# The order of residual, routing and bias products ahead of the expert loop of a hybrid decoder step

## The chip, the cores and the metric

The kernel runs on one core of one Trainium2 chip. The metric is device time in microseconds of one execution. TensorE (PE) multiplies matrices, VectorE (DVE) and ScalarE (ACT) work elementwise, GpSimd (POOL) does small odd jobs, SyncE (SP) issues the transfers. They run beside each other and meet at semaphores.

## The reference

One decoder layer for 256 prompt tokens and 32 new tokens (8 sequences of 4): norm, one projection, dilated attention beside a state-space mixer, output projection, residual, then a mixture of experts, residual, and a last norm. All in float32, D = 1024, 32 experts, 4 for each token. The part that matters here:

```python
logits = h @ w_router + b_router
top_v, top_i = lax.top_k(logits, 4);  gates = softmax(top_v)
# for each expert e and the tokens that chose it:
a = xb @ w1[e] + b1[e]                       # 1024 -> 2048
x_glu = minimum(a[:, :1024], 7);  x_lin = clip(a[:, 1024:], -7, 7)
mid = x_glu * sigmoid(1.702 * x_glu) * (x_lin + 1)
y  = mid @ w2[e] + b2[e]                     # 1024 -> 1024
out[token] += gate * y;   x = x + out;   y = rmsnorm(x) * norm_final_g
```

## The kernel before

Tokens lie in three tiles: 128 and 128 of the prompt, 32 samples (`TILES`). After the mixers comes the routing stage, then a loop over 32 experts. Each expert's weights are 12 pieces of 1 MB. There are 20 buffers for pieces (`NSLOT`); SP fills all of them with the pieces of the first experts before or during routing, and then refills a buffer each time the last block of its expert has used it (`refill`, L462 to L469). An expert works on its tokens in blocks of 32 (`CAP`), one pass of `pe_pass` each, 51 passes here. A pass gathers its tokens with a product against a selection matrix (L1572), multiplies by the first weights (`first_product`, L1592), by the second (`second_product`, L1600), and adds the block's rows to the output, which stays in PSUM banks 0 to 4 for the whole loop (`sum_back`, L1560 and L1562).

Experts are taken in an order by load: the two first are always experts 0 and 1, so that their weights can be fetched before routing is known; the others follow by their counts. Names, counts and running block numbers (`names_o`, `cnt`, `blk_n`) are read into registers by every engine that runs the loop.

The routing stage is one instruction stream for each engine, in the order of the code, with waits on semaphores. On PE: the transposes of the normed rows (L1486 to L1492), the logits (L1507), their stacking (L1512), the positions of the tokens within their expert (L1525), the counts as a row (L1528) and as a column (L1531), the gates transposed (L1535), the second bias times the gates (L1543, three groups by tile: `second_bias(0)`, `(2)`, `(1)`, with a wait between the last two), and the broadcast of names and counts to all partitions (L1548). Between them stand the products that put the residual rows x into the output banks with an identity matrix: `residual(q)` for quarter q of the columns (L1498, 512 wide, 128 rows), and four small ones for the samples (L1518, 256 wide, 32 rows). The bias products add to what the residual products wrote.

On DVE: the top-4 (L1065 to L1077, mask there at its end), the softmax (L1080 to L1083), the gates by expert (L1090), the positions by expert (L1101, L1103), the ranks and names (L1105 to L1111), the evictions of the broadcast (L1116 to L1123), and twice three copies that repeat the sample column of a table in all four quadrants of partitions (`in_all_quadrants`, L1094, for `gate` and `posm`). Then its loop begins: registers are read, and L1143 makes the first selection matrix.

Of the kernel before, what the change touches and what calls it, by code (L numbers as in the profile page):

```python
# [34 lines left out]
NS = NB * NSEQ  # L35
# [6 lines left out]
NEXP, TOPK, DFF = 32, 4, 1024  # L42
CAP = 32
NQ = D // (P // CAP)
# [76 lines left out]
def decoder_step(nc, I, O):  # L121

    with ExitStack() as ctx:
# [29 lines left out]
        ident = con[:, C_ID:C_ID + P]  # L153
# [5 lines left out]
        x = sb("x", [P, 3, D])  # L159
# [27 lines left out]
        posm = moe_buf(NEXP * 3).rearrange("p (e t) -> p e t", e=NEXP)  # L187
        gate = moe_buf(NEXP * 3).rearrange("p (e t) -> p e t", e=NEXP)
# [61 lines left out]
        ones = sb("ones", [P, P])  # L250
# [8 lines left out]
        rt_s = routing[:, 0:576].rearrange("p (t k e) -> p t k e", t=3, k=6)  # L259
# [7 lines left out]
        put = oh[0:NEXP, 0, :, :]  # L267
# [3 lines left out]
        ps = ctx.enter_context(nc.psum_tensor("ps", [P, 8, 512], F32))  # L271
# [10 lines left out]
        S = {n: sem("s_" + n) for n in names}  # L282
# [490 lines left out]
        def _(dve):  # L773
            chain = [0]

            def link(ins):

                chain[0] += 1
                ins.then_inc(S["chain_v"], 1)
                dve.wait_ge(S["chain_v"], chain[0])  # L780
# [11 lines left out]
            for t, (_, n) in enumerate(TILES):  # L792
                ins = ts(xn[0:n, t, :], x[0:n, t, :], st[0:n, 6 + t:7 + t], None, ALU.mult)
# [38 lines left out]
            q = lambda n: prm[:, n, :]  # L832
# [24 lines left out]
            for g in range(2):  # L857
# [3 lines left out]
                ins = tt(dst(1), s4(0)[rows], s4(1)[rows], ALU.add)  # L861
# [105 lines left out]
            for hh in range(H):  # L967
# [17 lines left out]
                if hh == 0:  # L985
                    sample_maxima(0)
                    dve.wait_ge(S["ysps"], 1)
                    for blk in range(4):
                        ins = stt(yS[:, blk, SEQ:], qkvu[:, 12 + blk, SEQ:], dsk[:, blk:blk + 1], ps[:, 2, NS * blk:NS * blk + NS], ALU.mult, ALU.add)
# [32 lines left out]
            for t, (_, n) in enumerate(TILES):  # L1022
                ins = ts(st[0:n, 36 + 2 * t:38 + 2 * t], ps[0:n, 5, 2 * t:2 * t + 2], 1.0 / 512, EPS, ALU.mult, ALU.add)
# [3 lines left out]
            for k, t in enumerate(SERVED):  # L1027
                n = TILES[t][1]
                dve.wait_ge(S["wo_ps"], k + 1)
                if t == 2:  # L1030
                    for a in range(2):
                        for c in range(2):
                            q = 64 * a + 32 * c
                            xv = x[0:n, t, 512 * c:512 * c + 512]
                            ins = stt(xv, ps[q:q + n, 4, :], st[0:n, 42 + 2 * t + a:43 + 2 * t + a], xv, ALU.mult, ALU.add)
# [17 lines left out]
                ins = dve.reciprocal(st[:, 54 + t:55 + t], st[:, 51 + t:52 + t])  # L1053
# [9 lines left out]
            lg, masks, es = rt_s[:, :, 0, :], rt_s[:, :, 1, :], rt_s[:, :, 2, :]  # L1063
            for t, (_, n) in enumerate(TILES):
                ins = stt(lg[0:n, t, :], ps[0:n, 6, 32 * t:32 * t + 32], st[0:n, 54 + t:55 + t], bro[0:n, :], ALU.mult, ALU.add)  # L1065
            link(ins)
            for t, (_, n) in enumerate(TILES):
                ins = dve.max(top[0:n, t, 0:8], lg[0:n, t, :])
            link(ins)
            for t, (_, n) in enumerate(TILES):  # L1070
                ins = dve.max_index(tidx[0:n, t, :], top[0:n, t, 0:8], lg[0:n, t, :])
# [14 lines left out]
            def by_expert(table, u, n):  # L1086
                return table[0:n, :, u].rearrange("p e t -> p t e")

            for u, n in ((slice(0, 2), P), (slice(2, 3), NS)):
                ins = dve.tensor_copy(by_expert(gate, u, n), es[0:n, u, :])  # L1090

            def in_all_quadrants(table):
                for q in range(1, 4):
                    ins = dve.tensor_copy(table[32 * q:32 * q + 32, :, 2], table[0:NS, :, 2])  # L1094
                return ins

            link(ins)
            in_all_quadrants(gate)

            dve.wait_ge(S["posps"], 1)  # L1100
            link(stt(rt_s[:, :, 3, :], ps[:, 7, 0:96].rearrange("p (t e) -> p t e", t=3), 1.0, masks, ALU.add, ALU.mult))  # L1101
# [8 lines left out]
            ts(put[:, 2, :], put[:, 1, :], name_col, None, ALU.mult)  # L1110
            ts(put[:, 3, :], put[:, 1, :], ps[0:NEXP, 7, 128:129], None, ALU.mult).then_inc(S["gates"], 1)  # L1111

            link(in_all_quadrants(posm))

            dve.wait_ge(S["gT_ps"], 2)
            dve.tensor_copy(names_o[:, :], ps[:, 7, 192:224])  # L1116
            ts(cnt[:, :], ps[:, 7, 224:256], 1.0, None, ALU.max).then_inc(S["cntr"], 1)
# [3 lines left out]
            link(ts(nblk[:, 0, :], nblk[:, 0, :], -ROUND, None, ALU.add))  # L1121
            link(dve.tensor_tensor_scan(nblk[:, 1, :], ones[:, 0:NEXP], nblk[:, 0, :], 0.0, ALU.mult, ALU.add))
            ts(blk_n[:, :], nblk[:, 1, :], -1.0, None, ALU.add).then_inc(S["blks"], 1)  # L1123

            def gating(n):

# [53 lines left out]
        def _(pe):  # L1180
            mm, tp = pe.matmul, pe.transpose
# [16 lines left out]
            for a, src in enumerate((par[0:NI, 0:P], par[0:NI, P:2 * P], st_out[0:NI, 0, :], st_out[0:NI, 1, :])):  # L1198
                ins = tp(ps[:, 0, NI * a:NI * a + NI], src, ident[0:NI, 0:NI])
# [3 lines left out]
            for r in range(2):  # L1203
                for b in range(4):
                    tp(ps[:, 2 + r, P * b:P * b + P], cnat[:, r, b, :], ident)
                ins = tp(ps[:, 1, P * r:P * r + P], h0row[:, r, :], ident)
# [21 lines left out]
            for r in range(2):  # L1228
                for b in range(4):
                    ins = tp(ps[:, r, P * b:P * b + P], xb[:, r, P * b:P * b + P], ident)  # L1230
# [163 lines left out]
            for i in range(NI):  # L1394
                blk, q = i // 4, 32 * (i % 4)
                for r in range(2):
                    ins = mm(ps[q:q + 32, 2, NS * blk:NS * blk + NS], cT[:, r, P * blk + q:P * blk + q + 32], hs[:, r, i, :],
                             start=(r == 0), stop=(r == 1), skip_group_check=True)
# [24 lines left out]
            for r in range(2):  # L1423
                tp(ps[0:NI, 1, P * r:P * r + P], hf[:, r, :], ident)
                ins = tp(ps[:, 1, SEQ + P * r:SEQ + P * r + P], sf[:, r, :], ident)
# [11 lines left out]
            for half in range(2):  # L1437
                for hp in range(4):
                    own = ident.rearrange("p (b r) -> p b r", b=4)[:, :, 8 * hp:8 * hp + 8]
                    at = P * half + 32 * hp  # L1440
                    ins = mm(ps[:, 0, at:at + 32], o_s[half][:, P * hp:P * hp + P], own, start=True, stop=True)
# [49 lines left out]
            for j in range(J):  # L1491
                ins = tp(ps[:, 4 + j // 4, P * (j % 4):P * (j % 4) + P], h[:, 1, j::J], ident)  # L1492
                if j % 4 == 3:
                    ins.then_inc(S["hT_ps"], 1)

            def residual(q):

                mm(ps[:, q, :].rearrange("p (t n) -> p t n", t=2), ident, x[:, 0:2, NQ * q:NQ * q + NQ], start=True, stop=True, skip_group_check=True)  # L1498

            pe.wait_ge(S["xT_a"], 4 + 4)  # L1500
            residual(0)
            pe.wait_ge(S["xT_a"], 4 + 5)
            pe.wait_ge(S["xT_d"], 4 + 1)
            for k in range(2):
# [1 line left out]
                    j = 4 * k + q  # L1506
                    ins = mm(ps[32 * q:32 * q + 32, 5, 0:NTOK], wr[:, j, :], accT[:, j, :], start=(k == 0), stop=(k == 1), skip_group_check=True)  # L1507
            ins.then_inc(S["lgT"], 1)
            residual(1)
            pe.wait_ge(S["lgs"], 1)  # L1510
            for t, (t0, n) in enumerate(TILES):
                ins = mm(ps[0:n, 6, 32 * t:32 * t + 32], lgT[:, t0:t0 + n], stack, start=True, stop=True)  # L1512
            ins.then_inc(S["lg"], 1)

            residual(2)
            residual(3)
            for q in range(4):
                mm(ps[32 * q:32 * q + 32, 4, 0:NQ], ident[0:NS, 0:NS], x[0:NS, 2, NQ * q:NQ * q + NQ], start=True, stop=True, skip_group_check=True)  # L1518

            pe.wait_ge(S["mask"], 1)  # L1520
            for t, (t0, n) in enumerate(TILES):
# [3 lines left out]
                    mm(ps[0:n, 7, 32 * t:32 * t + 32], w, rt_s[0:m, u, 1, :], start=(u == 0), stop=(u == t))  # L1525
            for u in range(3):
                m = TILES[u][1]
                ins = mm(ps[0:NEXP, 7, 96:128], ones[0:m, 0:NEXP], rt_s[0:m, u, 1, :], start=(u == 0), stop=(u == 2))  # L1528
            for u in range(3):
                m = TILES[u][1]  # L1530
                ins = mm(ps[0:NEXP, 7, 128:129], rt_s[0:m, u, 1, :], ones[0:m, 0:1], start=(u == 0), stop=(u == 2))  # L1531
            ins.then_inc(S["posps"], 1)
            pe.wait_ge(S["gates"], 1)
            for t, (t0, n) in enumerate(TILES):
                ins = mm(ps[NEXP * t:NEXP * t + NEXP, 6, 0:n], rt_s[0:n, t, 2, :], ident[0:n, 0:n], start=True, stop=True)  # L1535
            ins.then_inc(S["gT_ps"], 1)
            pe.wait_ge(S["gT"], 1)
            pe.wait_ge(S["b2"], 16 * 7)
            def second_bias(t):
                e0, n = NEXP * t, TILES[t][1]  # L1540
                for q in range(4):
                    out = ps[:, q, NQ * t:NQ * t + NQ] if t < 2 else ps[32 * q:32 * q + 32, 4, 0:NQ]
                    ins = mm(out, gT[e0:e0 + NEXP, 0:n], b2_rows[e0:e0 + NEXP, NQ * q:NQ * q + NQ], start=False, stop=True, skip_group_check=True)  # L1543
                ins.then_inc(S["comb"], 1)

            second_bias(0)
            pe.wait_ge(S["gates"], 2)
            mm(ps[:, 7, 192:256], ones[0:NEXP, :], put[:, 2:4, :], start=True, stop=True).then_inc(S["gT_ps"], 1)  # L1548
            second_bias(2)
            pe.wait_ge(S["comb"], 2)  # L1550
            second_bias(1)
            pe.wait_ge(S["cntr"], 1)

            def quarter(q):
# [121 lines left out]
```

## Time and profile before

| | us |
|---|---|
| median of 3 executions | 1273.71 (1271.83 to 1274.16) |
| profiled execution | 1274.16 |
| its span | 1272.4 |
| PE busy | 1103.0 (87%) |
| DVE busy | 428.0 (34%) |
| ACT busy | 212.4 (17%) |
| transfers, mean over the span | 350 GB/s, 442.46 MB read |
| mean granted clock of PE | 0.948 of full speed |

The page gives the busy time of each engine and a strip of 40 equal slices. The chain of waits runs back from the last instruction: PE 52%, transfers 18%, SP's queue 11%, DVE 10%. A timeline row has the start in us from the span's start, the length in us, the engine, the line of the code, the operation with out<-in by the program's names, rows*columns of the weights, the shape, and the number of instructions; a float32 product is two instructions, a transpose one. In brackets stands the idle time before it and what ended it. A windows row has the stretch, its length, the busy time of PE, of its weight loads (PEld), DVE, ACT and POOL with their number of instructions, the granted clock of PE (1.00 is 2.4 GHz), the busy share of the transfer engines, and GB/s. A row of the chain has start, length, engine, output and line. `ps` is PSUM, `x` the residual rows, `uni`, `low`, `ring`, `accT`, `tmp` and `kv_rows` are on-chip memory that is used in turn for several tables and for weights.

### The profile page before, as it was taken

How to read it: one execution, taken by the hardware profiler on the slowest of the kernel's cores; microseconds unless marked ns; L12 is line 12 of the kernel's file. 1: busy time of each engine (PE TensorE's matmuls, PEld its weight loads, DVE VectorE, ACT ScalarE, POOL GpSimd, SP SyncE). 2: the span in 40 equal slices, each digit the busy share in tenths (PEclk: the TensorE clock that was granted, in tenths of full speed). 3: DMA queues.
4: the chain of work that ended last, by engine and by line, in shares of the span. 5: the costliest groups of instructions: out<-in, count | busy, mean ns of one | idle time of the engine just before them, and what ended most of it. 6: DMA issues, size and time to landing. Idle time of an engine off the chain costs nothing.

```text
span 1272.4 us, 30002 instructions
## 1 busy us (share of the span) xinstructions
PE 1103.0 (87%) x10851; PEld 501.5 (39%) x10852; DVE 428.0 (34%) x1361; ACT 212.4 (17%) x377; POOL 80.5 (6%) x189
## 2 busy tenths in 40 slices
PE   5999788999988799989898877699899968998985
PEld 4765444453433244433343332243344412443332
DVE  4999853642222222222222211122222211222121
ACT  3102433230111111111111100011111110111112
POOL 2268400000000000000000000000000000000000
PEclk9999998989998899999999988899899998999897
DMA  8424692970799999999999999999999999999995
GB/s 245 159 83 146 190 332 93 391 303 18 303 419 420 420 415 374 419 421 382 419 421 420 420 420 420 420 369 419 421 419 384 420 419 420 385 419 420 420 420 221
DMA packets 81108, 446.25 MB, mean 351 GB/s; under 512 B 16768, under 2 KB 18112, under 8 KB 32256
## 3 DMA queue, kind: packets, MB, share of 16 engines
q1 hardware_dynamic: 81024, 445.00, 86.9%
q8 instruction: 68, 1.11, 0.4%
q14 instruction: 16, 0.13, 0.0%
HBM read 442.46 MB, written 2.51 MB: 350 GB/s over the span
## 4 chain that ended last, share of the span: by engine, by line
PE 52%; DMA 18%; SPq 11%; DVE 10%; issue 4%; ACT 1%; POOL 0%; DVEq 0%; ACTq 0%
PE ps L1592 20%; DMA ring<-in_w_moe_dram 11%; SPq L469 10%; PE ps L1600 10%; DMA low<-in_w_moe_dram 5%; PE ps L1572 4%; PE ps L1562 3%; PE ps L1585 3%; DMA w_glu<-in_w_moe_dram 2%; PE ps L1462 2%; PE ps L1580 1%; PE ps L1560 1%; PE ps L1617 1%; PE ps L1622 1%; DVE ring L892 1%
## 5 line engine op out<-in xcount | busy, mean ns | idle before, releaser
L1592 PE MATMUL ps<-ring,uni 128*32 128x512 f32 x2032 | 252.9, 636 | 76.0 <-issue 51.6
L1592 PEld LDWEIGHTS ps<-ring,uni 128*32 128x32 f32 x2032 | 63.9, 114 | 254.8 <-issue 205.2
L1128 DVE TENSOR_SCALAR uni<-ps 128x256 f32<-128x256 f32 x51 | 21.7, 425 | 336.6 <-PE ps L1592 336.6
L1600 PE MATMUL ps<-ring,uni 128*32 128x256 f32 x1792 | 105.8, 381 | 7.9 <-DMA ring<-in_w_moe_dram 7.9
L753 ACT ACTIVATE uni<-uni 128x256 f32<-128x256 f32 x51 | 21.2, 416 | 436.3 <-DVE uni L1128 436.3
L1150 DVE COPY uni<-ps 128x256 f32<-128x256 f32 x51 | 21.7, 425 | 214.4 <-PE ps L1580 214.4
L1572 PE MATMUL ps<-uni 128*32 128x256 f32 x1248 | 82.7, 401 | 0.0
L753 ACT ACT_TABLE_LOAD x51 | 65.4, 1283 | 89.3 <-issue 89.3
L1600 PEld LDWEIGHTS ps<-ring,uni 128*32 128x32 f32 x1792 | 54.6, 110 | 48.5 <-DMA ring<-in_w_moe_dram 11.7
L1221 PE MATMUL ps<-accT,ring 128*128 128x288 f32 x256 | 66.0, 413 | 0.0
L1562 PE MATMUL ps<-uni 32*128 32x256 f32 x832 | 62.9, 418 | 0.0
L1562 PEld LDWEIGHTS ps<-uni 32*128 32x128 f32 x832 | 39.5, 194 | 48.4 <-issue 46.8
L1585 PE MATMUL ps<-uni 32*32 32x512 f32 x416 | 55.1, 600 | 0.0
L1221 PEld LDWEIGHTS ps<-accT,ring 128*128 128x128 f32 x256 | 48.1, 192 | 15.6 <-issue 3.3
L1572 PEld LDWEIGHTS ps<-uni 128*32 128x32 f32 x1248 | 36.5, 113 | 38.7 <-issue 22.2
L1143 DVE TENSOR_TENSOR uni<-low,uni 128x96 f32 x51 | 13.2, 259 | 112.7 <-issue 103.0
L755 ACT ACTIVATE uni<-ps 128x384 f32<-128x384 f32 x51 | 25.0, 491 | 149.5 <-PE ps L1622 149.5
L757 ACT ACTIVATE uni<-ps 128x256 f32<-128x256 f32 x51 | 19.6, 385 | 176.1 <-PE ps L1600 176.1
L1137 DVE COPY uni<-ps 128x256 f32<-128x256 f32 x51 | 21.7, 425 | 69.9 <-PE ps L1617 69.9
L1155 DVE TENSOR_TENSOR uni<-uni 128x64 f32<-128x64 f32 x204 | 44.5, 218 | 1.4
L1592 PE MATMUL ps<-tmp,uni 128*32 128x512 f32 x320 | 41.8, 641 | 1.4 <-DMA tmp<-in_w_moe_dram 1.4
L1156 DVE TENSOR_TENSOR uni<-uni 32x32 f32<-32x32 f32 x204 | 37.0, 182 | 2.1
(378 smaller groups left out, 1287.2 us busy)
## 6 DMA issues: line engine op xcount, KB each, us to landing
ring<-in_w_moe_dram SPq DMA_DIRECT2D x232, 1024.0 KB, 24.5
tmp<-in_w_moe_dram SPq DMA_DIRECT2D x38, 1024.0 KB, 26.0
kv_rows<-in_w_moe_dram SPq DMA_DIRECT2D x19, 1024.0 KB, 23.4
w_glu<-in_w_moe_dram SPq DMA_DIRECT2D x19, 1024.0 KB, 26.7
mixer<-in_w_moe_dram SPq DMA_DIRECT2D x19, 1024.0 KB, 25.1
uni<-in_w_moe_dram SPq DMA_DIRECT2D x19, 1024.0 KB, 26.2
accT<-in_w_moe_dram SPq DMA_DIRECT2D x19, 1024.0 KB, 26.5
low<-in_w_moe_dram SPq DMA_DIRECT2D x19, 1024.0 KB, 26.9
```

The source lines that it names most:

```text
L469: sp.dma_start(slot(turn, k), piece(following[later - 1], k2)).then_inc(landed(turn, k), 16)
L753: A(sig, glu_b, ACT.Sigmoid, scale=ALPHA).then_inc(S["sgm"], 1)
L755: A(selT, ps[:, 5, 0:3 * P], ACT.Copy).then_inc(S["selT"], 1)
L1155: tt(selg[:, 0:2, q, :], sel[:, 0:2, :], gb[:, 0:2, :], ALU.mult)
L1156: ins = tt(selg[rows, 2, q, :], sel[rows, 2, :], gb[rows, 2, :], ALU.mult)
L1221: ins = mm(ps[:, 4 + n % 2, 0:NTOK], w_in[:, c // 4, j, P * (c % 4):P * (c % 4) + P], accT[:, j, :], start=(j == 0), stop=(j == J - 1))
L1462: ins = mm(ps[:, 4 * t + 2 * a + c, :], src[:, kb, t0:t0 + P], w_out[:, 4 * a + kb, 512 * c:512 * c + 512], start=(kb == 0), stop=(kb == 3))
L1562: ins = mm(ps[:, q, NQ * t:NQ * t + NQ], selT[quarter(q), P * t:P * t + P], y[quarter(q), :], start=False, stop=True, skip_group_check=True)
L1572: ins = mm(ps[quarter(q), 6, 0:NQ], sel[:, t, :], h[:, t, NQ * q:NQ * q + NQ], start=(t == 0), stop=(t == 2), skip_group_check=True)
L1585: mm(hidden(q), pick[quarter(q), :], b1_rows[quarter(q), :].rearrange("p (g n) -> p g n", g=2), start=True, stop=False, skip_group_check=True)
L1592: ins = mm(hidden(q), xe[:, k % 2, quarter(k // 2)], slot(turn, k)[:, :, NQ * q:NQ * q + NQ], start=False, stop=(k == 7), skip_group_check ...
L1600: ins = mm(ps[quarter(q), 7, 0:NQ], mt[:, m, quarter(k - 8)], slot(turn, k)[:, m, NQ * q:NQ * q + NQ], start=(k == 8 and m == 0), stop=(k ...
```

## The change

On PE, `residual(q)` takes the sample product of its quarter with it (four small products, one behind each wide one, where they stood together). Residual 0 and 1 go behind the stacked logits (ahead of the mask), residual 2 and 3 behind the counts (ahead of the transposed gates). The broadcast of names and counts goes ahead of all bias products, and the three bias groups follow each other. The wait of residual 0 on ACT's copies goes. The row of counts is made for 128 partitions where it was made for 32. On DVE the six copies of `in_all_quadrants` go from two places to one behind `blk_n`, and DVE waits for the last of them before its loop.

```diff
             for u, n in ((slice(0, 2), P), (slice(2, 3), NS)):
-                ins = dve.tensor_copy(by_expert(gate, u, n), es[0:n, u, :])
-            def in_all_quadrants(table):
-                for q in range(1, 4):
-                    ins = dve.tensor_copy(table[32 * q:32 * q + 32, :, 2], table[0:NS, :, 2])
-                return ins
-            link(ins)
-            in_all_quadrants(gate)
+                dve.tensor_copy(by_expert(gate, u, n), es[0:n, u, :])
...
-            link(in_all_quadrants(posm))
...
             ts(blk_n[:, :], nblk[:, 1, :], -1.0, None, ALU.add).then_inc(S["blks"], 1)
+            for table in (gate, posm):
+                for q in range(1, 4):
+                    ins = dve.tensor_copy(table[32 * q:32 * q + 32, :, 2], table[0:NS, :, 2])
+            link(ins)
...
-            pe.wait_ge(S["xT_a"], 4 + 4)
-            residual(0)
...
-            residual(1)
...
-            residual(2)
-            residual(3)
-            for q in range(4):
+            def residual(q):
+                mm(ps[:, q, :].rearrange("p (t n) -> p t n", t=2), ident, x[:, 0:2, NQ * q:NQ * q + NQ], start=True, stop=True, skip_group_check=True)
                 mm(ps[32 * q:32 * q + 32, 4, 0:NQ], ident[0:NS, 0:NS], x[0:NS, 2, NQ * q:NQ * q + NQ], start=True, stop=True, skip_group_check=True)
+            residual(0)
+            residual(1)
...
-                ins = mm(ps[0:NEXP, 7, 96:128], ones[0:m, 0:NEXP], rt_s[0:m, u, 1, :], start=(u == 0), stop=(u == 2))
+                ins = mm(ps[:, 7, 96:128], ones[0:m, :], rt_s[0:m, u, 1, :], start=(u == 0), stop=(u == 2))
...
             ins.then_inc(S["posps"], 1)
+            residual(2)
+            residual(3)
             pe.wait_ge(S["gates"], 1)
...
+            pe.wait_ge(S["gates"], 2)
+            mm(ps[:, 7, 192:256], ones[0:NEXP, :], put[:, 2:4, :], start=True, stop=True).then_inc(S["gT_ps"], 1)
...
-            second_bias(0)
-            pe.wait_ge(S["gates"], 2)
-            mm(ps[:, 7, 192:256], ones[0:NEXP, :], put[:, 2:4, :], start=True, stop=True).then_inc(S["gT_ps"], 1)
-            second_bias(2)
-            pe.wait_ge(S["comb"], 2)
-            second_bias(1)
+            for t in (0, 2, 1):
                 e0, n = NEXP * t, TILES[t][1]
+                if t == 1:
+                    pe.wait_ge(S["comb"], 2)
```

PE before, from the residual product ahead of the logits to the first product for the positions (`x` is the residual, `accT` the transposed rows, `low` and `uni` hold constants and logits):

```order
L1498 MATMUL ps<-x,low 128x512
L1507 MATMUL ps<-accT,low 32x288 x8
L1498 MATMUL ps<-x,low 128x512
L1512 MATMUL ps<-low,uni 128x32 x2
L1512 MATMUL ps<-low,uni 32x32
L1498 MATMUL ps<-x,low 128x512 x2
L1518 MATMUL ps<-x,low 32x256 x4
L1525 MATMUL ps<-low 128x32
```

And the same stretch of PE in the changed kernel (its line numbers are lower by about ten; L1504 and L1505 are the two products of a residual quarter):

```order
L1495 MATMUL ps<-accT,low 32x288 x8
L1499 MATMUL ps<-low,uni 128x32 x2
L1499 MATMUL ps<-low,uni 32x32
L1504 MATMUL ps<-x,low 128x512
L1505 MATMUL ps<-x,low 32x256
L1504 MATMUL ps<-x,low 128x512
L1505 MATMUL ps<-x,low 32x256
L1515 MATMUL ps<-low 128x32
```

Two quarters instead of four stand ahead of the positions, and none ahead of the stacked logits. PE before, from the counts to the gather of the first block (`gT` the transposed gates, `kv_rows` the second bias):

```order
L1528 MATMUL ps<-low,ones 32x32 x3
L1531 MATMUL ps<-ones,low 32x1 x3
L1535 MATMUL ps<-low 32x128 x2
L1535 MATMUL ps<-low 32x32
L1543 MATMUL ps<-kv_rows,gT 128x256 x4
L1548 MATMUL ps<-low,ones 128x64
L1543 MATMUL ps<-kv_rows,gT 32x256 x4
L1543 MATMUL ps<-kv_rows,gT 128x256 x4
L1572 MATMUL ps<-uni 32x256 x12
```

And in the changed kernel, where L1530 is the broadcast, L1540 the bias and L1562 the gather:

```order
L1521 MATMUL ps<-ones,low 32x1 x3
L1504 MATMUL ps<-x,low 128x512
L1505 MATMUL ps<-x,low 32x256
L1504 MATMUL ps<-x,low 128x512
L1505 MATMUL ps<-x,low 32x256
L1527 MATMUL ps<-low 32x128 x2
L1527 MATMUL ps<-low 32x32
L1530 MATMUL ps<-low,ones 128x64
L1540 MATMUL ps<-kv_rows,gT 128x256 x4
L1540 MATMUL ps<-kv_rows,gT 32x256 x4
L1540 MATMUL ps<-kv_rows,gT 128x256 x4
L1562 MATMUL ps<-uni 32x256 x12
```

Two residual quarters now stand ahead of the transposed gates, and the broadcast ahead of the bias. DVE in the changed kernel from the eviction of the names to the start of its loop (L1117 are the six copies, which stood as twice three behind L1090 and L1111):

```order
L1106 CAST names_o<-ps 128x32
L1107 TENSOR_SCALAR cnt<-ps 128x32
L1109 TENSOR_SCALAR nblk<-ps 128x32
L1110 TENSOR_SCALAR nblk<-nblk 128x32
L1111 TENSOR_SCALAR nblk<-nblk 128x32
L1112 SCALAR_TENSOR_TENSOR nblk<-ones,nblk 128x32
L1113 TENSOR_SCALAR blk_n<-nblk 128x32
L1117 COPY uni<-uni 32x32 x6
L338 UNCONDITIONAL_BRANCH
L338 ISA
L325 TENSOR_LOAD cnt
```

The copies stand between the block numbers and the reading of the counts into registers.

## Rows read from the trace of the kernel before

**Rows 1.** Page, strip of 40 slices of 31.8 us: GB/s moved

```profile
GB/s 245 159 83 146 190 332 93 391 303 18 303 419 420 420 415 374 419 421 382 419 421 420 420 420 420 420 369 419 421 419 384 420 419 420 385 419 420 420 420 221
```

**Rows 2.** Timeline of the transfer queue (SP), first refill

```profile
325.37 7.40 SPq L469 DMA_DIRECT2D ring<-in_w_moe_dram  x8
```

**Rows 3.** Chain of waits, third run of first products: start, length, what

```profile
324.16 7.00 PE ps L1592 x64
```

**Rows 4.** Timeline of PE, from the logits to the first block

```profile
267.16 1.18 PE L1507 MATMUL ps<-accT,low 128*32 128x288 f32 x16
...
269.23 0.71 PE L1512 MATMUL ps<-low,uni 128*128 128x32 f32 x6
269.86 1.98 PE L1498 MATMUL ps<-x,low 128*128 128x512 f32 x4
271.78 0.63 PE L1518 MATMUL ps<-x,low 32*32 32x256 f32 x8
273.46 0.41 PE L1525 MATMUL ps<-low 128*128 128x32 f32 x2 [1.05 <-DVE low L1077]
273.71 0.39 PE L1525 MATMUL ps<-low,ones 128*128 128x32 f32 x2
273.93 0.39 PE L1525 MATMUL ps<-low 128*128 128x32 f32 x2
...
274.66 0.48 PE L1528 MATMUL ps<-low,ones 128*32 128x32 f32 x6
275.08 0.43 PE L1531 MATMUL ps<-ones,low 128*32 128x1 f32 x6
275.44 0.59 PE L1535 MATMUL ps<-low 128*32 128x128 f32 x6
276.59 3.12 PE L1543 MATMUL ps<-kv_rows,gT 32*128 32x256 f32 x8 [0.56 <-ACT gT L750]
279.51 0.52 PE L1548 MATMUL ps<-low,ones 32*128 32x64 f32 x2
279.96 4.94 PE L1543 MATMUL ps<-kv_rows,gT 32*32 32x256 f32 x16
284.83 2.79 PE L1572 MATMUL ps<-uni 128*32 128x256 f32 x24
...
291.00 8.72 PE L1592 MATMUL ps<-ring,uni 128*32 128x512 f32 x64 [1.26 <-issue]
299.64 1.15 PE L1562 MATMUL ps<-uni 32*128 32x256 f32 x16
```

**Rows 5.** Timeline of DVE over the same stretch

```profile
266.25 0.69 DVE L1057 COPY accT<-ps 128x512 f32<-128x512 f32 x1 [0.78 <-PE ps L1492]
268.40 0.46 DVE L1060 COPY uni<-ps 128x288 f32<-128x288 f32 x1 [1.46 <-PE ps L1507]
...
272.61 0.80 DVE L1077 TENSOR_REDUCE low<-low 128x96 f32<-128x384 f32 x1
...
274.85 0.57 DVE L1094 COPY uni<-uni 32x32 f32<-32x32 f32 x3
275.55 0.26 DVE L1101 SCALAR_TENSOR_TENSOR low<-ps,low 128x96 f32<-128x96 f32 x1
...
277.20 0.23 DVE L1111 TENSOR_SCALAR low<-low,ps 32x32 f32<-32x32 f32 x1
...
280.14 0.19 DVE L1116 CAST names_o<-ps 128x32 int32<-128x32 f32 x1 [2.11 <-PE ps L1548]
...
284.32 0.26 DVE L1143 TENSOR_TENSOR uni<-low,uni 128x96 f32 x1 [2.88 <-issue]
```

**Rows 6.** Windows table, all engines: around the fall, then two stretches

```profile
277.00:277.50 0.50, 0.50 (x4) 0.40 (x3) 0.43 (x4) 0.00 (x0) 0.00 (x0) 0.80 1.01 426
277.50:287.50 10.00, 9.91 (x48) 5.56 (x46) 2.09 (x12) 1.28 (x1) 0.00 (x0) 0.50 0.95 378
291.00:294.00 3.00, 3.00 (x16) 0.81 (x20) 0.26 (x1) 0.00 (x0) 0.00 (x0) 0.50 0.00 0
```

More of the change, by code:

```diff
@@ L1494, in _ @@
                     ins.then_inc(S["hT_ps"], 1)
-            def residual(q):
-                mm(ps[:, q, :].rearrange("p (t n) -> p t n", t=2), ident, x[:, 0:2, NQ * q:NQ * q + NQ], start=True, stop=True, skip_group_check=True)
-            pe.wait_ge(S["xT_a"], 4 + 4)
-            residual(0)
             pe.wait_ge(S["xT_a"], 4 + 5)
@@ L1536, in _ @@
             ins.then_inc(S["gT_ps"], 1)
+            pe.wait_ge(S["gates"], 2)
+            mm(ps[:, 7, 192:256], ones[0:NEXP, :], put[:, 2:4, :], start=True, stop=True).then_inc(S["gT_ps"], 1)
             pe.wait_ge(S["gT"], 1)
             pe.wait_ge(S["b2"], 16 * 7)
-            def second_bias(t):
+            for t in (0, 2, 1):
                 e0, n = NEXP * t, TILES[t][1]
+                if t == 1:
+                    pe.wait_ge(S["comb"], 2)
                 for q in range(4):
```

## Prediction

> **What bounds the kernel now.** I first read the strip of the page with the GB/s of 40 slices, then the transfer queue's own timeline, then the chain of waits, and last the timelines of TensorE (PE) and VectorE (DVE) around 266 to 300 us. The strip [rows 1] shows about 420 GB/s in nearly every slice from 350 us on, so the expert weights set the pace of the last 900 us; but one slice, the tenth (286 to 318 us), shows 18 GB/s. By then all twenty weight buffers are full, and none comes free before the last block of tokens of the first expert has used it: the first refill is issued at 325.37 [rows 2], 1.2 us after the third run of first products starts at 324.16 [rows 3]. All weight traffic behind that hangs on this point, and that point hangs on the start of the first expert block, L1592 at 291.00 [rows 4]. The three blocks up to it find their weights on chip, so they run at PE's own pace. So whatever the routing stage gains or loses up to the first block reaches the end one to one, and what it does behind that to the transfers in flight costs nothing: the channel is empty from 289 us on anyway. The term to forecast is therefore one: how much earlier or later L1592 starts.
>
> Going back from 291.00 on the PE timeline [rows 4]: the gather of the first block, L1572, starts at 284.83, straight behind the second-bias products L1543, whose last group ends at 279.96 + 4.94 = 284.90. The other thing the gather waits for, the selection matrix of DVE (L1143), starts at 284.32 and takes 0.26, so it is there at 284.58 [rows 5]. PE's own queue is last by 0.3 us, with DVE right behind it: a gain on PE alone is worth at most 0.3 us.
>
> **The change part by part.** (1) Residual products 0 and 1 leave the places ahead of the logits (L1507) and ahead of L1512. Each was about 1 us of PE: 1.98 us for two [rows 4]. The last input of L1507 is there at 266.25 + 0.69 = 266.94, it starts at 267.16 [rows 4, 5]; I take back 0.15. L1512 starts at 269.23 though its input is there at 268.40 + 0.46 = 268.86; with a weight load in between I take back another 0.15. From there to the mask the way is DVE's alone, so the mask, now there at 272.61 + 0.80 = 273.41, comes at 273.1. Bounds: 0 and 0.22 + 0.37 = 0.6 earlier.
>
> (2) The count product L1528 loads 128 columns where it had 32. The nearest rows are L1525: starts with 128 columns stand 0.25 and 0.22 us apart (273.46, 273.71), the three products of L1528 take 0.42 (274.66 to 275.08), 0.14 each. So 3 x 0.08 = 0.24 later; bounds 0 and 3 x 0.27. With (1) the positions are ready at 275.45, where now DVE goes on at 275.55 (L1101). Its two sets of three copies go behind the counts; the first set (0.57 us, ended 275.42) stood beside PE's work and is worth nothing there. The naming chain on DVE (L1101 to L1111, over at 277.43) thus ends at 277.35, unchanged.
>
> The Trainium skill (TensorE: Matmul & The Clock Gate, LDWEIGHTS) says that a weight load costs its number of columns over 1.2 GHz, whatever the rows; as an estimate from that page the six loads cost 6 x 0.08 = 0.48 us, and the sum would be 0.24 us worse. The rows have half of that, since half of each load lies behind the product before it.
>
> (3) Residual products 2 and 3, each now with one 32-row product behind it, stand behind the positions and ahead of the transposed gates (L1535). At full clock a pair costs 0.99 + 0.3 (the four 32-row products took 0.63 side by side [rows 4]; each alone is one 256-wide product, bounded by 0.16 and by 0.43); I take 1.28 for a pair. Products 0 and 1 fit between L1512 and the mask: 269.6 to 272.1, with 273.1 wanted; that cover is 1.0 us thick at full clock and gone at half. Products 2 and 3 are on the path: 275.3 to 277.9. Then the transposed gates, 0.59, to 278.5; ScalarE's copy to the next PE start, 0.56 [rows 4]; the bias products start at 279.0, where now they start at 276.59. This is +2.4 us.
>
> (4) The broadcast of names and counts (L1548) moves ahead of all bias products, to 278.5 to 278.8; now it ends at 280.03. DVE's read of it (L1116, now 280.14) comes at 278.9. From there to L1143 are 284.32 - 280.14 = 4.18 us, mostly the read of counts into registers; the six copies (2 x 0.57, and the wait for the last) now stand in that stretch ahead of the register reads, +1.2. L1143 starts at 278.9 + 4.2 + 1.2 = 284.3: unchanged, and this is the floor under the gather, 284.55. The earlier names are eaten by the copies. The other engines get their counts 1.2 us earlier and wait for others anyway; the one fill that SP issues on it lands in the empty stretch.
>
> (5) The bias products themselves. Now they take 3.12 + 4.94 us, and most of that at the lower clock: the windows [rows 6] show the granted clock at 0.80 of 2.4 GHz in 277.0 to 277.5 and at 0.50 (1.2 GHz) until 287.5. It fell at 277.2, while PE was busy with small products and the first bias ones, 5.4 us after the last 512-wide residual product (269.86 + 1.98). At full clock the first group would be 0.6 + 2.5/2 = 1.9 and the last two 4.94/2 = 2.5; the group for the samples, whose four products go side by side, is about a fifth of the 2.5, 0.5. New in the order is that the sample group follows the first one with nothing between; it uses other rows of the array, and eight such 32-row products of L1562 on four row groups took 1.15 [rows 4], so they can run side by side. I take half of its cost away (bounds: none, all). That leaves 4.1 us at full clock, 8.2 at half. The fall may come as far behind the last wide product as before, at 277.9 + 5.4 = 283.3, or as early as their start at 279.0; I take 280.9, about the middle. Then 1.9 us are done and the other 2.2 take 4.4: end at 285.3, against 284.90.
>
> Sum: the last bias product ends at 285.3 against 284.9, and the gather shifts with it, +0.4 us. What follows the gather (copy, transpose, register reads, 291.00) keeps its length. The profiled execution was 1274.16 with a span of 1272.4; it becomes 1274.6. That execution is the slowest of three with median 1273.71, so the median becomes 1274.1. What a measurement of this kernel can tell from no change is about 0.2%, 2.5 us.
>
> **The rivals.** *A: the clock falls before the late residual products.* Between 272.1 and 275.3 PE now has only small products and a pause of 1.0 us. In the kernel before that pause was 1.05 us and the small products ran at full clock, but the fall came 5.4 us behind the last wide product; where the fall comes relative to the program I can't tell from one trace. If it comes in this gap, products 2 and 3 take 5.1 instead of 2.6 and reach to 280.6, gates and copy end at 282, and bias products at half clock throughout end at 290: +5. If the wide residual products at half clock bring the clock back, as L1572 did at 287.5, about half of this stays: +2 to +3. I take +3, 1276.7. It decides from the point where the fall comes earlier than 277. For it: the new order has a thinner stretch than before there. Against it: the fall seen came later than 277, and products 2 and 3 are wide ones.
>
> *B: the clock stays full.* The wide products stand 3.5 us closer to the bias products than before. If it holds to the end of them, they end at 279.0 + 4.1 = 283.1, the gather starts at DVE's floor 284.55, -0.3, takes 1.4 instead of 2.79, and the first expert block, 8.72 us with half clock in 291 to 294 [rows 4, 6], takes 7.0: in all -3.4 us, 1270.3. Against it: small and 32-row products are what PE did when the clock fell, with hardly a pause.
>
> The Trainium skill (the same page, Why this matters for your kernels) ties the loss of clock to idle gaps of PE between bursts. PE has no long gap here in either kernel, so by that rule the clock would stay up and B is the forecast. The trace disagrees: PE was busy for 9.91 of 10.00 us at clock 0.50. I leave it little.
>
> *C: the change is absorbed.* If the first refill did not hang on the first block, nothing would reach the end: 1273.7, the same. The timeline speaks against it, and it can't be told from the forecast by time alone.
>
> **How the numbers follow.** Forecast with its neighbourhood (gather from -0.3 to +2.2 us, C included): 0.70, 1271.5 to 1276.3. A: 0.18. B, whole or nearly: 0.07. What is left, 0.05, goes to a gain of another kind, such as the clock in the first expert block, which can change by 1.7 us either way. Faster by over 0.2% is B and the rest, 0.12; slower is A, 0.18; within 0.70. The range for 8 in 10 goes from 1271.5 to 1276.8.
>
> **What would show it.** Mask ready about 0.3 us earlier; PE residual pairs behind the positions, 2.6 us long at clock 1; names on DVE 1.2 us earlier but L1143's counterpart at the same time; bias products starting 2.4 us later and ending within 0.5 us of 284.9; DVE's six copies in the stretch ahead of the register reads; the refill at 325.4 + 0.4. I am wrong if the residual pairs run at clock 0.5 (A), if bias products take 4 us and the first block 7 (B), or if the first refill doesn't move with the first block (C).

## The result: 9.5 us slower, outside the range

The changed kernel takes 1283.12 us (median, 1282.13 to 1283.71), against 1273.65 before: ratio 1.0085, interval 1.0063 to 1.0107. I had forecast 1274.1, no change, with 1271.5 to 1276.8 for 8 in 10. Timed again it was 1281.76 against 1272.38, ratio 1.0080 (1.0062 to 1.0098).

The page of the changed kernel has the same work and the same instruction count; the strip shows where the end moved (columns as in [rows 1], slices of 32.0 us):

```profile
span 1281.8 us, 30002 instructions
GB/s 246 155 83 142 193 352 88 396 238 54 206 419 420 421 420 370 420 421 420 382 419 421 421 420 419 421 368 420 421 419 380 420 420 420 386 418 422 419 420 227
```

The eleventh slice has 206 GB/s where [rows 1] has 303: the weights start again later. The transfer queue and the chain of waits say by how much:

```profile
335.20 7.40 SPq L469 DMA_DIRECT2D ring<-in_w_moe_dram  x8
...
302.47 7.07 PE ps L1582 x64
...
333.99 7.00 PE ps L1582 x64
```

First refill 335.20, was 325.37 [rows 2]; third run of first products 333.99, was 324.16 [rows 3]: both +9.83. The first expert block starts at 302.47, was 291.00 [rows 4]: +11.47, of which it gives back 1.65 (7.07 instead of 8.72, as it runs at full clock now). The span is 9.4 us longer, 0.4 less than the shift of the refill. So the loss lies ahead of 302.47. The timeline of PE there, to be laid beside [rows 4]:

```profile
264.19 1.16 PE L1487 MATMUL ps<-low,uni 128*128 128x128 f32 x8
266.30 2.15 PE L1495 MATMUL ps<-accT,low 128*32 128x288 f32 x16 [0.94 <-DVE accT L1057]
...
270.25 2.08 PE L1504 MATMUL ps<-x,low 128*128 128x512 f32 x2
272.26 1.06 PE L1505 MATMUL ps<-x,low 32*32 32x256 f32 x2
273.25 2.08 PE L1504 MATMUL ps<-x,low 128*128 128x512 f32 x2
275.25 1.06 PE L1505 MATMUL ps<-x,low 32*32 32x256 f32 x2
276.24 0.64 PE L1515 MATMUL ps<-low 128*128 128x32 f32 x2
...
278.25 1.62 PE L1518 MATMUL ps<-low,ones 128*128 128x32 f32 x6
279.81 0.57 PE L1521 MATMUL ps<-ones,low 128*32 128x1 f32 x6
280.31 2.07 PE L1504 MATMUL ps<-x,low 128*128 128x512 f32 x2
...
286.29 0.89 PE L1527 MATMUL ps<-low 128*32 128x128 f32 x6
287.10 0.68 PE L1530 MATMUL ps<-low,ones 32*128 32x64 f32 x2
287.73 8.64 PE L1540 MATMUL ps<-kv_rows,gT 32*128 32x256 f32 x24
296.31 2.79 PE L1562 MATMUL ps<-uni 128*32 128x256 f32 x24
```

And the windows table over the same stretch (columns as in [rows 6]):

```profile
255.00:265.50 10.50, 10.35 (x37) 5.92 (x35) 4.11 (x6) 3.37 (x12) 0.00 (x0) 1.00 0.31 90
265.50:266.30 0.80, 0.00 (x1) 0.04 (x2) 0.65 (x1) 0.80 (x2) 0.00 (x0) 0.69 0.93 358
266.30:299.50 33.20, 32.14 (x118) 15.18 (x118) 9.61 (x49) 5.82 (x8) 0.00 (x0) 0.50 0.63 253
300.00:310.00 10.00, 8.76 (x82) 2.74 (x85) 2.44 (x12) 0.00 (x0) 0.00 (x0) 1.00 0.01 2
```

Where residual product 0 stood, PE now pauses 0.94 us for DVE's copy. Within that pause the granted clock falls from 1.00 to 0.50: the mean of 0.69 over 0.80 us puts the fall at 265.8. It then stays at 0.50 (1.2 GHz) for 33 us though PE is busy for 32.14 of them. Before, it fell only at 277.3 (0.80 over 277.0 to 277.5 [rows 6]).

The 11.14 us by which the bias products start later (287.73 against 276.59 [rows 4]) come apart like this. The transposes end 0.80 earlier in this execution (265.35 against 266.15). From there to the mask, now at 273.80 (DVE row below), it is 8.45 us instead of 7.26: +1.2, logits at half clock. The mask's products then wait until 276.24 for residual pairs 0 and 1, 3 us each: +2.4. Positions and counts take 4.1 instead of 2.0: +2.1. Pairs 2 and 3: +6.0. Gates and copy: +0.3. That is 12.0, less the 0.8 of the earlier start: 11.2, against 11.14 read directly.

DVE's timeline, beside [rows 5]:

```profile
273.00 0.80 DVE L1077 TENSOR_REDUCE low<-low 128x96 f32<-128x384 f32 x1
...
280.41 0.26 DVE L1093 SCALAR_TENSOR_TENSOR low<-ps,low 128x96 f32<-128x96 f32 x1 [5.21 <-PE ps L1521]
...
287.82 0.19 DVE L1106 CAST names_o<-ps 128x32 int32<-128x32 f32 x1 [5.53 <-PE ps L1530]
...
289.14 1.15 DVE L1117 COPY uni<-uni 32x32 f32<-32x32 f32 x6
293.37 0.26 DVE L1138 TENSOR_TENSOR uni<-low,uni 128x96 f32 x1 [3.07 <-issue]
```

Names to selection matrix are 5.55 us, 4.18 before plus copies; the matrix is there 2.7 us before PE is done with the bias. So DVE is not what holds up the gather.

### The profile page after: what moved, and what is told of

Read it like the earlier page. It is cut to its first block, busy times and chain, and to the rows that moved or that the text cites. A ratio compares the mean times of both kernels' runs of the same rounds, so it can differ in the third digit from the quotient of the medians.

```text
span 1281.8 us, 30002 instructions
## 1 busy us (share of the span) xinstructions
PE 1109.1 (87%) x10851; PEld 504.3 (39%) x10852; DVE 427.3 (33%) x1361; ACT 212.4 (17%) x377; POOL 81.2 (6%) x189
## 4 chain that ended last, share of the span: by engine, by line
PE 51%; DMA 20%; SPq 14%; DVE 8%; issue 5%; ACT 1%; POOL 1%; DVEq 0%; ACTq 0%
PE ps L1582 19%; SPq L469 11%; PE ps L1590 9%; DMA low<-in_w_moe_dram 7%; DMA ring<-in_w_moe_dram 7%; DMA w_glu<-in_w_moe_dram 5%; PE ps L1562 4%; PE ps L1575 3%; PE ps L1552 3%; PE ps L1457 2%; DMA ring<-in_w_in_dram 2%; PE ps L1570 1%; PE ps L1216 1%; PE ps L1550 1%; PE ps L1607 1%
## 5 line engine op out<-in xcount | busy, mean ns | idle before, releaser
L1582 PE MATMUL ps<-ring,uni 128*32 128x512 f32 x2032 | 249.5, 629 | 75.8 <-issue 55.0
L1562 PE MATMUL ps<-uni 128*32 128x256 f32 x1248 | 80.1, 391 | 0.0
L1562 PEld LDWEIGHTS ps<-uni 128*32 128x32 f32 x1248 | 35.8, 111 | 37.0 <-issue 19.8
```

Of the source, the lines that this page charges most:

```text
L1562: ins = mm(ps[quarter(q), 6, 0:NQ], sel[:, t, :], h[:, t, NQ * q:NQ * q + NQ], start=(t == 0), stop=(t == 2), skip_group_check=True)
L1582: ins = mm(hidden(q), xe[:, k % 2, quarter(k // 2)], slot(turn, k)[:, :, NQ * q:NQ * q + NQ], start=False, stop=(k == 7), skip_group_check ...
```

## The experiments

After the result I held this theory (theory 1 in the expectations): the product ahead of the logits keeps the clock up, since transposes alone don't. The main rival was that the late residual products and the new order cost by themselves. Each ratio is against the kernel before, run on the same chip; PE rows of changed versions are quoted where a verdict rests on them.

**The changed kernel again** (`a_again`).

> The changed kernel itself again, in more executions. Theory 1 (transposes do not hold the clock, so it nearly always falls ahead of the logits once the wide product there is gone): most executions lie at 1281 to 1284 and the profile shows the fall between 264 and 267. Rival (the fall ahead of the logits was an accident of the first executions): the median comes to 1276 to 1279, near that of the kernel with the wide product put back (1277.0).

1281.76, ratio 1.0080 (1.0062 to 1.0098). Its profile has the fall in the same pause, at another time of the execution (263.1 to 264.0, the stage being 2.2 us earlier). So the fall was no accident of one execution.

**Residual product 0 out of the pause, in the kernel before** (`b_res0_behind`).

```diff
-            pe.wait_ge(S["xT_a"], 4 + 4)
-            residual(0)
...
+            residual(0)
             residual(2)
             residual(3)
```

> The kernel before with one thing changed: residual product 0 (wide, 128 rows) no longer stands between the transposes and the logits, but with 2 and 3 behind the stacked logits. Theory 1 (the wide product ahead of the logits is what keeps TensorE's clock up over the stretch of transposes): the granted clock falls to 0.50 near 266 instead of 277, the logits take about 2.1 us instead of 1.2, bias products start 2 to 5 us later and all run at half clock, total 3 to 6 us above before. Rival (the loss comes from the late residual products and their order alone): clock falls near 277 as before, total within 1.5 us of before.

1273.62, ratio 1.0014 (0.9998 to 1.0031), 1.2 us by the medians and no clear loss; my 3 to 6 us were wrong. But its windows have both the fall in the pause and a return:

```profile
266.00:266.70 0.70, 0.00 (x0) 0.00 (x0) 0.59 (x1) 0.70 (x2) 0.00 (x0) 0.84 0.86 339
266.80:269.90 3.10, 3.10 (x18) 1.16 (x19) 0.46 (x1) 3.08 (x4) 0.00 (x0) 0.50 1.01 423
270.00:276.00 6.00, 5.80 (x39) 3.12 (x37) 4.51 (x23) 0.83 (x2) 0.00 (x0) 1.00 1.01 426
```

So the pause brings the fall, but here the fall costs little: the clock is back after 3.4 us, at 269.9, within the wide residual product 1, which follows straight behind the logits. In the changed kernel it isn't. Two things are needed for the 9.5 us.

**A wide product put back into the pause** (`a_wide_ahead`).

```diff
+            pe.wait_ge(S["xT_a"], 4 + 4)
+            mm(ps[:, 0, :]..., ident, x[:, 0:2, 0:NQ], ...)
             pe.wait_ge(S["xT_a"], 4 + 5)
```

> The changed kernel with one wide product (128 rows x 512 columns) added between the transposes and the logits; it writes bank 0, which residual product 0 overwrites later, and only costs its 1 us. Theory 1: the granted clock stays at 1.00 past 266, residual pairs take 1.3 us each instead of 3.1, the time comes back to 1273 to 1276. Rival (the new order costs 9 us by itself, the clock is a bystander): stays at 1282 to 1284.

1277.01, ratio 1.0033 (1.0019 to 1.0047). An added product of 1 us takes about 5 us off. The clock holds to 276.7, residual pairs 0 and 1 take 1.6 us each and leave the mask alone. But 4.6 us of loss remain (2.4 to 6.0 by the interval), more than theory 1 had. The PE timeline shows where: the clock falls just ahead of residual 3.

```profile
275.25 1.12 PE L1506 MATMUL ps<-x,low 128*128 128x512 f32 x2
276.31 0.66 PE L1507 MATMUL ps<-x,low 32*32 32x256 f32 x2
276.89 2.08 PE L1506 MATMUL ps<-x,low 128*128 128x512 f32 x2
278.90 1.06 PE L1507 MATMUL ps<-x,low 32*32 32x256 f32 x2
```

From there on all runs at half clock up to 293.8, the bias products (8.65 us) included.

**Eight transposes in the pause** (`a_transposes_x`).

```diff
+            pe.wait_ge(S["xT_a"], 4 + 4)
+            for j in range(J):
+                tp(ps[:, j // 4, P * (j % 4):P * (j % 4) + P], x[:, 1, j::J], ident)
```

> The changed kernel with eight more transposes of residual rows (128 x 128, about 1.1 us, result overwritten later) where the run with the wide product had that product. Both keep TensorE busy up to the logits. If it is busy time that holds the clock, the total comes to about 1277 as with the wide product, and the clock falls near 276. If transposes don't hold it, the clock falls at 263 to 267 as in the changed kernel and the total stays at 1281 to 1284.

1277.85, ratio 1.0039 (1.0025 to 1.0053): the same cure. My reason is refuted: transposes hold the clock as a wide product does. The Trainium skill (TensorE: Matmul & The Clock Gate, Part 4: PE-mode transpose) says that full clock doesn't engage for transposes, since they don't count as busy in the same way. If that held here, the run would have stayed near 1282. The measurement decides: float32 transposes held a clock that was already up. Whether they would also raise it, no run here shows.

**Thin products in the pause** (`a_thin_ahead`): two of 32 x 32 weights, 256 wide.

```diff
+            pe.wait_ge(S["xT_a"], 4 + 4)
+            for _ in range(2):
+                mm(ps[0:32, 0, 0:NQ], ident[0:NS, 0:NS], x[0:NS, 2, 0:NQ], ...)
```

> The changed kernel with two products of 32 rows and 32 columns of weights (256 wide, 0.43 us each, result overwritten later) in the pause ahead of the logits. If busy time of any kind holds the clock, as the transposes did: about 1277, fall near 277. If only products that use the whole array (wide ones and full transposes) hold it: the fall stays at 263 to 267 and the total at 1281 to 1284.

1276.94, ratio 1.0033 (1.0022 to 1.0044). The windows before, in and after the filled pause:

```profile
255.00:265.40 10.40, 10.40 (x37) 5.99 (x35) 4.06 (x5) 3.12 (x12) 0.00 (x0) 1.00 0.33 106
265.40:266.40 1.00, 1.00 (x5) 0.34 (x4) 0.69 (x1) 1.00 (x3) 0.00 (x0) 1.00 0.96 377
266.40:276.80 10.40, 9.50 (x60) 4.85 (x60) 6.41 (x33) 4.13 (x5) 0.00 (x0) 0.99 1.01 426
```

At this place it is the pause, not what fills it. In the profiles, the clock fell in it in all four with the pause open (two of the changed kernel, `b_res0_behind`, `a_narrow_last`) and in none of the twelve with it filled.

**The narrow products together behind the last wide one** (`a_narrow_last`), pause open.

```diff
             def residual(q):
                 mm(ps[:, q, :]..., ident, x[:, 0:2, NQ * q:NQ * q + NQ], ...)
-                mm(ps[32 * q:32 * q + 32, 4, 0:NQ], ident[0:NS, 0:NS], x[0:NS, 2, ...], ...)
...
             residual(2)
             residual(3)
+            for q in range(4):
+                mm(ps[32 * q:32 * q + 32, 4, 0:NQ], ident[0:NS, 0:NS], x[0:NS, 2, ...], ...)
```

> The changed kernel with its four narrow products (32 rows) together behind residual 3, so that wide products 0 and 1 follow each other. Without a narrow product between them the wide pair should bring the clock back by about 273, as in the run where residual 0 stood behind the logits (clock back at 270): the mask products start 2 us earlier, and the total is 3 to 6 us under 1283. If narrow products between do no harm to the clock, only the 2 us that the pair no longer holds up the mask products go: 1281.

1277.75, ratio 1.0038 (1.0020 to 1.0056), 4 us under the changed kernel timed beside it, where 2 us are what the narrow products no longer take ahead of the mask. Its PE timeline and windows:

```profile
266.20 2.15 PE L1495 MATMUL ps<-accT,low 128*32 128x288 f32 x16 [0.94 <-DVE accT L1057]
...
270.16 3.29 PE L1504 MATMUL ps<-x,low 128*128 128x512 f32 x4
```

```profile
266.20:272.40 6.20, 5.63 (x25) 2.95 (x26) 2.38 (x16) 3.80 (x4) 0.00 (x0) 0.50 1.01 425
272.50:276.00 3.50, 3.18 (x24) 2.03 (x22) 2.41 (x8) 0.23 (x1) 0.00 (x0) 0.95 1.01 426
```

The fall in the pause is still there, but with two wide products in a row the clock is back at 272.8 (0.95 over 272.5 to 276.0), while with pairs of wide and narrow it stayed at 0.50 to 299.9. That is the second half, shown by one profile against two of the changed kernel: the 32 x 32 products between the wide ones kept the clock down once it was down. It did not stay up for good: it fell again at 276.2, was back at 279.6, and fell once more at 283.1, in the bias products. A narrow product also is work of its own: four in a row took 0.63 us side by side, four apart take 0.5 us each at full clock and 1 us at half.

**Both cures** (`a_wide_narrow_last`).

> The changed kernel with both cures: the wide product ahead of the logits and the narrow products together behind residual 3. If both work on the clock they add up in part: clock up until 277 to 280, bias starting near 279, total 1273 to 1276. If the late place of residual 2 and 3 is what costs the rest, it stays near 1277.

1273.62, ratio 1.0021 (1.0004 to 1.0038). The clock holds to 279.8, bias starts at 278.72 and takes 7.61, first block at 292.36. What is left of the change is 1.0 us by the medians, 0.5 to 4.8 by the interval. I put it down to the late place of residual 2 and 3, the wider counts and the copies; no run takes them apart here. One more row of it matters. PE pauses for 1.6 us ahead of the mask, and the clock stays up:

```profile
271.00:272.60 1.60, 0.02 (x1) 0.00 (x0) 1.53 (x3) 0.28 (x1) 0.00 (x0) 1.00 1.02 430
```

So a pause doesn't bring the clock down by its length alone. This one stands behind two wide products, the one of 0.94 us behind 5.3 us of transposes.

**Residual 2 and 3 late, alone, in the kernel before** (`b_res23_late`).

> The kernel before with residual products 2 and 3 and the four sample products moved behind the counts (wide product 0 still ahead of the logits). Theory 1: clock stays up to about 277 or longer, bias starts about 2.5 us later, total 0 to +3 us. Rival 2 (the late pairs are what loses: wide products at half clock): total +5 us or more, residual products of 2 us each.

1277.27, ratio 1.0038 (1.0023 to 1.0052): nearly +5, on the rival's side. Its PE timeline says why:

```profile
271.59 0.71 PE L1512 MATMUL ps<-low,uni 128*128 128x32 f32 x6
275.82 0.48 PE L1520 MATMUL ps<-low 128*128 128x32 f32 x2 [3.53 <-DVE low L1077]
...
278.77 3.78 PE L1498 MATMUL ps<-x,low 128*128 128x512 f32 x4
```

Moving them away opens a pause of 3.53 us ahead of the mask, the clock falls right behind it (276.0), and the wide products run at half clock. From their start to the transposed gates it is 4.43 us (278.77 to 283.20); the same products in the same place took 2.47 at full clock, in the run with both cures (275.10 to 277.57), where residual 0 and 1 leave a pause of only 1.62. So about 2 us of it are the clock and 2.5 the late place itself; in the run with both cures that price is partly hidden by what the higher clock gives back further on (first block in 7.07 us, 8.72 before). That the long pause is what brought the fall is likely, but no run fills it alone.

**Names early and copies late, alone** (`b_names_copies`), and **counts on 128 partitions, alone** (`b_counts128`).

> The kernel before with only the broadcast of names ahead of the bias and the six copies of VectorE behind the block numbers. By my step 4 names come about 1.5 us earlier, the copies eat 1.2 of it, bias starts up to 0.7 us later (the broadcast waits for the naming chain at 277.4): total 0 to +1.5 us. If one of them is what costs, +4 us or more.

> The kernel before with only the row of counts made for 128 partitions. By the row of the kernel with the wide product (0.96 us for these three products at full clock against 0.48) the positions come 0.5 us later: total 0 to +0.5 us, no change that a measurement tells. If the longer weight loads bring the clock down earlier: +2 us or more.

1272.43, ratio 0.9999 (0.9990 to 1.0009), and 1272.91, ratio 1.0006 (0.9996 to 1.0017): no clear part of the loss. At full clock the three count products take 0.96 us with 128 columns (here and in `a_wide_ahead`) against 0.48 with 32 [rows 4].

**A faster version** (`b_bias_pairs`, and again as `b_pairs_again`): the kernel before, names ahead of the bias, and the bias of tile 0 and tile 1 issued in pairs that use different rows of the array and different banks.

```diff
+            pe.wait_ge(S["gates"], 2)
+            mm(ps[:, 7, 192:256], ones[0:NEXP, :], put[:, 2:4, :], ...)
...
-            second_bias(0)
-            pe.wait_ge(S["gates"], 2)
-            mm(ps[:, 7, 192:256], ones[0:NEXP, :], put[:, 2:4, :], ...)
-            second_bias(2)
-            pe.wait_ge(S["comb"], 2)
-            second_bias(1)
...
+            def bias_pair(q):
+                bias_product(0, q)
+                return bias_product(1, (q + 2) % 4)
...
+            bias_pair(0)
+            bias_pair(1).then_inc(S["comb"], 1)
+            for q in range(4):
+                ins = bias_product(2, q)
+            ins.then_inc(S["comb"], 1)
+            pe.wait_ge(S["comb"], 1)
+            bias_pair(2)
+            bias_pair(3).then_inc(S["comb"], 1)
```

> A try at a faster kernel: before with the broadcast of names ahead of the bias products, and the bias products of the two prompt tiles issued in pairs on different row groups and banks (tile 0 quarter q with tile 1 quarter q+2), one wait between the two halves. If 32-row products on different row groups run side by side, bias takes 4 to 5 us at half clock instead of 8, the gather starts at about 282 to 283 and the total is 1.5 to 2.5 us below before. If they do not, the bias takes 8 us from 277.5 on and the total is 0 to 1 us above before.

> The paired-bias kernel once more on the same chip as the one with three extra products, for the comparison: 1270 again, 2 to 2.5 us below before.

1270.12, ratio 0.9979 (0.9967 to 0.9991), and 1268.18, ratio 0.9967 (0.9955 to 0.9979): faster than both kernels. The bias is shorter at half clock (0.50 from 276.9 to 290.5):

```profile
277.64 5.03 PE L1544 MATMUL ps<-kv_rows,gT 32*128 32x256 f32 x23
282.60 2.79 PE L1578 MATMUL ps<-uni 128*32 128x256 f32 x24
```

Twelve products in about 5.4 us (277.27 to 282.67) instead of 8.64, and DVE's selection matrix at 282.12 + 0.26 = 282.38: the two engines are even again, 2.2 us earlier than in [rows 4], of which 0.3 are the earlier logits of this execution (266.84 against 267.16).

**Unused wide products in the pauses of that version** (`b_pairs_extra` with four, `b_pairs_extra1` with three).

> The paired-bias kernel (1270.1) with four extra wide products whose result is never used (bank 5), put where TensorE only waits: one ahead of the mask, one behind the transposed gates, two behind the bias. If wide products hold the clock up, bias takes 2.5 to 3 us instead of 5, the gather 1.4 instead of 2.8 and the first block starts at full clock: total 1266 to 1268.5. If they don't, the extra work costs 0 to 4 us: 1270 to 1274.

> The paired-bias kernel with three extra wide products (one behind the bias instead of two; with two, the gather waited for them until 281.8 though VectorE was ready earlier). Expected: gather about 1 to 1.7 us earlier than with two, clock mostly up: 1267.5 to 1269. If the clock falls more often without the second one: 1269 to 1270.5, no better than without any extra product.

1269.39, ratio 0.9979 (0.9970 to 0.9989), and 1270.28, ratio 0.9979 (0.9966 to 0.9992), the second 2 us above the version without extras on the same chip. Neither brought the gain that I expected. They work on the clock: in the profile with four it is at 0.50 only from 278.4 to 281.8, and 23 of the 24 bias instructions take 2.70 us instead of 5.03. It buys no time that the ratios show: the gather starts at 281.80, straight behind the last two unused products, which run mostly at half clock themselves (3.63 us). From the start of the bias products to the gather it is 6.4 us (275.44 to 281.80), against 5.3 without extras (277.27 to 282.60).

## Why the prediction was wrong

- **The frame held.** I said that one term decides, the start of the first expert block, and that it reaches the end one to one. Span less that start is 981.4 before, 979.3 after, and lies between 978.7 and 981.8 in all 16 profiles, while the start itself goes from 286.6 to 302.5.
- **The step that failed is (1).** I priced the removal of residual product 0 as a gain of 0.15 us and named only the work it had delayed, not what it did itself: it filled the wait for DVE's copy. Leaving its place empty costs 4 to 5 us in the changed kernel (1281.8 against 1276.9 to 1277.9 with any product in the pause). I had the pause in my own numbers, 266.15 to 266.94, and looked only at how soon the logits could start.
- **The term for the fall in (5) failed with it, and so did (3).** I let the clock fall between 279.0 and 283.3, as far behind the last wide product as before or at the start of the bias. It fell at 265.8. I had priced a residual pair at 1.28 us; it took 1.60 at full clock (`a_wide_ahead`) and 3.0 at half, so that the two pairs behind the counts, 2.6 in my sum, took 6.0.
- **Rival A had the right mechanism in the wrong place.** It put the fall between the residual batches, 272 to 275.3, took +3, and gave it 0.18. The fall came at 265.8, so that the logits, both batches, and the small products all ran at half clock. With the pause filled, rival A is what happened: the clock fell at 276.7, just ahead of residual 3, and 4.6 us were lost; the rival had +5 with the clock down throughout, and +2 to +3 with a return. I had written that the cover of pairs 0 and 1 is "1.0 us thick at full clock and gone at half"; at half they held the mask products for 2.4 us.
- **"If the wide residual products at half clock bring the clock back" was half right.** Two in a row did (`a_narrow_last`), one straight behind the logits did (`b_res0_behind`), wide and narrow pairs didn't. The narrow products I had priced at 0.3 us each. With the pause open their places cost 4 us of the total (1281.8 to 1277.75). With it filled the medians give 3.4 (1277.0 to 1273.6), the ratios only 1.5 (1.0033 to 1.0021), and these two intervals overlap.
- **Step (2)**: the counts cost 0.48 more, not 0.24. I had rejected the estimate from the Trainium skill (TensorE: Matmul & The Clock Gate, LDWEIGHTS) for half of it; the runs have the 0.48 that it gives, as an estimate for six loads. The loss of the total doesn't hang on it.
- **Step (4)** was right in its length, names to selection matrix 5.55 against my 5.4, and alone it costs nothing (ratio 0.9999).
- **Step (5)**: I took half of the sample group's cost away for running beside the first group. All three groups took 8.64 us at half clock, against 8.2 forecast: no sign of that overlap. With two row groups in alternation throughout it does happen (`b_bias_pairs`).
- **Rival B** (clock stays full) and its rule on idle gaps: no run kept the clock up over the whole stage, but the direction of the rule was a warning that I read wrongly. That PE is busy for 9.91 of 10.00 us at 0.50 [rows 6] says nothing of what stood ahead of the fall: in the kernel before, a pause of 0.56 us ended 0.7 us ahead of it (276.59 [rows 4]). The Trainium skill (same page, Why this matters for your kernels) ties losses of clock to idle gaps; I answered that there was no long gap. A pause of 0.94 us was enough here, behind the transposes.

What stays open: why pauses of 1.05 us (the kernel before) and 1.62 us ahead of the mask leave the clock up while one of 0.94 us behind the transposes doesn't; why 32 x 32 products between wide ones keep the clock down while the same products fill a pause well enough to keep it up; and how often the fall misses an open pause (it did not in four profiles, though single executions of `b_res0_behind` lie between 1271.1 and 1280.0).

## What to carry to other kernels

A product that seems to be in the way of the critical product may be what bridges a wait. Before it is moved, look at whether PE is idle where it stood, and price the half clock for everything that follows up to the next dense stretch, not just the pause. To bridge the pause any product served here, narrow ones and transposes too; to bring the clock back, wide products in a row did it and mixed ones didn't. So the small products on one corner of the array are better kept together, side by side, behind the wide ones. Not every pause brings the clock down, so look in the trace at what it does there.

## What the runs showed of the hardware that I had not expected

- A pause of 0.94 us behind 5.3 us of transposes took the clock to 1.2 GHz in four of four profiles, and in the changed kernel it stayed there for 33 us with PE busy 97% of the time. A pause of 1.62 us behind two wide products (`a_wide_narrow_last`) did not.
- With the pause filled, by a wide product, transposes or 32 x 32 products alike, the clock held for another 10 us (to 276.7, 277.8 and 276.7).
- Twelve bias products of 32 rows took 5.4 us at 1.2 GHz with eight of them in alternation on two row groups and different banks, against 8.64 group by group. Row groups and banks were changed together; no run takes them apart.
